# Conditioning matrix in slabs of 1024 columns, its blocks in pairs, and the head loops written out

## The reference

```python
cs = jax.nn.silu(c)
for i in range(DEPTH):
    mod = cs @ ada_w[i] + ada_b[i]                      # 9 x 12288, ada_w[i] is 2048 x 12288
    sh1, sc1, g1, sh2, sc2, g2 = jnp.split(mod, N_ADA, axis=-1)
    h = rmsnorm(x, norm_mix_g[i]) * (1.0 + sc1[:, None]) + sh1[:, None]
    out = retention(h, ...) if i == 0 else pool_mixer(h, ...)
    x = x + g1[:, None] * out
    h = rmsnorm(x, norm_ffn_g[i]) * (1.0 + sc2[:, None]) + sh2[:, None]
    x = x + g2[:, None] * swiglu(h, ffn_w_in[i], ffn_w_out[i])
return rmsnorm(x, final_norm_g), ...
```

## Time and profile before

| | us |
|---|---|
| median of 3 runs | 3572.06 (3571.36 to 3572.34) |
| the profiled execution | 3572.51 |
| its span, first to last instruction | 3570.9 |

### The profile page before, as it was taken

The page is one execution under the profiler, slowest core; times in us unless marked ns, Lnnn a source line. Parts: engine busy times, 40 slices in busy tenths (PEclk is TensorE's granted clock), DMA queues, the critical chain, the costliest instruction groups (busy, mean ns, idle before and its releaser), DMA issues.

```text
span 3570.9 us, 61767 instructions
## 1 busy us (share of the span) xinstructions
PE 3371.0 (94%) x23530; PEld 3048.3 (85%) x23530; DVE 1737.4 (49%) x2763; ACT 1068.4 (30%) x1334; POOL 105.2 (3%) x152
## 2 busy tenths in 40 slices
PE   6799999999999987999999999998499999999997
PEld 2588888888888876899999999988489999999997
DVE  0334463645537357344444444445845545455555
ACT  1233322232322223322322223323333333333332
POOL 0000000000000001000000000000100000000000
PEclk8699999999999997999999999999699999999998
DMA  9665767576675744766666666665154444454442
GB/s 330 227 222 190 252 216 251 182 252 222 212 253 195 254 173 162 243 208 211 211 211 211 212 211 212 228 219 166 59 202 152 147 148 151 147 148 152 147 149 98
DMA packets 191213, 699.63 MB, mean 196 GB/s; under 512 B 20432, under 2 KB 20688, under 8 KB 191088
## 3 DMA queue, kind: packets, MB, share of 16 engines
q1 hardware_dynamic: 170496, 619.26, 51.6%
q0 software_dynamic: 19440, 74.97, 6.2%
q10 hardware_dynamic: 1152, 3.56, 0.3%
HBM read 656.23 MB, written 41.48 MB: 195 GB/s over the span
## 4 chain that ended last, share of the span: by engine, by line
PE 88%; DVE 5%; DMA 3%; issue 2%; ACT 1%; POOL 0%; SPq 0%; DVEq 0%; POOLq 0%; ACTq 0%
PE pair L1199 27%; PE pair L1201 25%; PE pair L1200 25%; PE adab L1214 6%; DMA sb_raw<-in_ada_w 2%; DVE sb_w_lo L753 1%; PE m L1185 1%; DVE sb_big L1044 1%; PE m L1353 1%; DMA sb_raw<-in_ret_w_in 1%; PE m L1319 1%; PE m L1228 0%; PE m L1349 0%; DVE sb_X L882 0%; ACT sb_w_hi L538 0%
## 5 line engine op out<-in xcount | busy, mean ns | idle before, releaser
L753 DVE TENSOR_TENSOR sb_w_lo<-sb_raw,sb_w_hi 128x1024 fp32r<-128x1024 f32 x792 | 966.3, 1223 | 1367.9 <-ACT sb_w_hi L538 1364.8
L1199 PE MATMUL pair<-sb_h_hi,sb_w_hi 128*128 128x320 f32 x4416 | 1406.2, 318 | 50.0 <-DVE sb_h_lo L1108 32.1
L538 ACT ACTIVATE sb_w_hi<-sb_raw 128x1024 fp32r<-128x1024 f32 x792 | 837.8, 1060 | 2019.9 <-PE pair L1201 994.7
L1201 PE MATMUL pair<-sb_h_hi,sb_w_lo 128*128 128x320 f32 x4416 | 1370.8, 310 | 0.0
L1200 PE MATMUL pair<-sb_h_lo,sb_w_hi 128*128 128x320 f32 x4416 | 1370.3, 310 | 0.0
L1199 PEld LDWEIGHTS pair<-sb_h_hi,sb_w_hi 128*128 128x128 f32 x4416 | 835.8, 189 | 166.1 <-issue 119.3
L1200 PEld LDWEIGHTS pair<-sb_h_lo,sb_w_hi 128*128 128x128 f32 x4416 | 836.6, 189 | 0.0
L1201 PEld LDWEIGHTS pair<-sb_h_hi,sb_w_lo 128*128 128x128 f32 x4416 | 835.4, 189 | 0.0
L1199 PE MATMUL pair<-sb_y_hi,sb_w_hi 128*128 128x320 f32 x1920 | 602.6, 314 | 13.5 <-DVE sb_y_lo L1032 10.4
L1200 PE MATMUL pair<-sb_y_lo,sb_w_hi 128*128 128x320 f32 x1920 | 596.6, 311 | 0.0
L1201 PE MATMUL pair<-sb_y_hi,sb_w_lo 128*128 128x320 f32 x1920 | 596.3, 311 | 0.0
(11 more groups left out here) (158 smaller groups left out, 1325.5 us busy)
## 6 DMA issues: line engine op xcount, KB each, us to landing
sb_raw<-in_ada_w SPq DMA_DIRECT2D x384, 512.0 KB, 3.6
sb_raw<-in_ffn_w_in SPq DMA_DIRECT2D x352, 512.0 KB, 3.6
sb_raw<-in_ret_w_in SPq DMA_DIRECT2D x192, 512.0 KB, 4.9
sb_raw<-in_ffn_w_out SPq DMA_DIRECT2D x176, 512.0 KB, 3.6
sb_big<-in_state_ret POOLq DMA_DIRECT2D x32, 1024.0 KB, 8.7
sb_raw<-in_ret_w_out SPq DMA_DIRECT2D x64, 512.0 KB, 4.3
out_state_ret_sample<-sb_big POOLq DMA_DIRECT2D x32, 1024.0 KB, 6.4
out_state_ret_prompt<-sb_o_s POOLq DMA_DIRECT2D x8, 512.0 KB, 4.1
```

What stands on the lines that cost most here:

```text
L538: A(w_hi[s][:, :, :], raw[C.n["unit"] % RAW_SLOTS][:, :, :], ACT.Copy).then_inc(hi_done, 1)
L753: V.tensor_tensor(w_lo[s][:, :, :], raw[slot][:, :, :], w_hi[s][:, :, :].bitcast(F32), ALU.subtract)\
L1199: MM(out, wh, hi[:, c, :], start=first and k == 0, stop=False)
L1201: ins = MM(out, wl, hi[:, c, :], start=False, stop=last and k == BK - 1)
```

## The change

The conditioning matrix is laid out anew on the host (`in_slabs`): a conditioning block is now one chunk of 128 rows by 1024 columns. The four column groups take 256 columns each of the same chunk, and 16 blocks in a row complete a *slab* of 1024 columns, with no partial sums. ACT copies the bank once a slab; TensorE transposes the two halves (`turn_ada`) into the other half of the same bank; DVE adds the bias of eight chunks at once. For layer 0 shift and scale are interleaved in the first four slabs.

Conditioning blocks come in pairs behind weight blocks: behind every second one in the heads' first two laps and in the first feed-forward step of each layer (`EACH_SECOND`), behind every third one over all three laps in layer 0's steps 1 to 10 (`EACH_THIRD`). SP loads them in the order in which they are used. With `pend`, ACT copies behind its fourth split of a lap, TensorE turns behind the lap's first weight block, and DVE adds the bias behind its fifth split. In the heads this is the gate lap, in the feed-forward steps the first lap. TensorE's step F now waits for the bias addition, not the copy. The loops over heads 2 to 7 (1 to 6 on POOL) are written out on every engine. The diff, cut:

```diff
-ADA0 = 16
+SLAB = 8
+SLABS = 6 * DC // SLAB
+SLABS0 = 2 * DC // SLAB
...
+NONE = ()
+EACH_SECOND = (1, 3, 5, 7)
+EACH_THIRD = ((2, 5), (0, 3, 6), (1, 4, 7))
+
+
+def first_layer_order():
+
+    return [4 * q + (SH1, SC1)[part] + c for q in range(4) for part in range(2) for c in range(4)]
+
+
+def at_shift(c):
...
+            def load_ada(layer):
+
+                load("ada", block_of(a["ada_w"][layer], C("adas", -layer * SLABS), C.n["ada"] % DC))
+                if C.n["ada"] % DC == 0:
+                    C.n["adas"] += 1
+
+            def load_block(src, k=0, layer=0, pairs=NONE):
 
                 load("gemm", src)
-                if owed:
-                    load_ada(owed.pop())
-                if now:
-                    load_ada(ada)
-                elif ada is not None:
...
+                if k in pairs:
+                    load_ada(layer)
+                    load_ada(layer)
+
+            def load_k16(w, cols, layer=0, pairs=NONE):
                 for n in range(8):
-                    load_block(block_of(w, n % 4, cols[n // 4]), ada, now=end and n == 7)
-
-            def load_k4(w, row):
...
+            for _ in range(DC):
+                load_ada(0)
+            with C.loop(sp, 1, SLABS0, unit=DC, ada=DC, adas=1):
+                for _ in range(DC):
                     load_ada(0)
-            with C.loop(sp, 1, ADA0 // 2, unit=8, ada=8, adas=2):
-                for _ in range(8):
...
             def head(h, out):
-                load_k16(w_in, [h * 2 + VCOL // BN, h * 2 + (VCOL // BN + 1)], ada=0)
-                load_k16(w_in, [h + KCOL // BN, h + QCOL // BN], ada=0)
+                load_k16(w_in, [h * 2 + VCOL // BN, h * 2 + (VCOL // BN + 1)], 0, EACH_SECOND)
+                load_k16(w_in, [h + KCOL // BN, h + QCOL // BN], 0, EACH_SECOND)
                 load_k16(w_in, [h * 2 + GCOL // BN, h * 2 + (GCOL // BN + 1)])
                 if out:
                     load_k4(w_out, h - 1)
 
             head(0, False)
             head(1, True)
-            with C.loop(sp, 2, H, unit=48, gemm=32, ada=16, adas=4) as h:
+            for h in range(2, H):
                 head(h, True)
             load_k4(w_out, H - 1)
...
+            def feed_forward(layer, i, pairs):
                 w1, w2 = a["ffn_w_in"][layer], a["ffn_w_out"][layer]
-                load_k16(w1, [i * 2, i * 2 + 1], ada=ada)
-                if out:
-                    load_k4(w2, i - 1)
-                load_k16(w1, [i * 2 + DFF // BN, i * 2 + (DFF // BN + 1)], ada=ada, end=end)
-
-            feed_forward(0, 0, 1, out=False)
-            with C.loop(sp, 1, FF_STEPS, unit=40, gemm=24, ada=16, adas=4) as i:
-                feed_forward(0, i, 1)
+                load_k16(w1, [i * 2, i * 2 + 1], 1, pairs[0])
+                if len(pairs) == 3:
+                    load_k4(w2, i - 1, 1, pairs[1])
+                load_k16(w1, [i * 2 + DFF // BN, i * 2 + (DFF // BN + 1)], 1, pairs[-1])
+
+            feed_forward(0, 0, (EACH_SECOND, EACH_SECOND))
+            with C.loop(sp, 1, FF_STEPS, unit=40, gemm=24, ada=16, adas=1) as i:
+                feed_forward(0, i, EACH_THIRD)
...
             def copy_ada():
 
-                act.wait_ge(ada_done, C("adas") * 4 + 4)
+                act.wait_ge(ada_done, C("adas") * DC + DC)
                 if C.n["adas"]:
-                    act.wait_ge(ada_folded, C("adas"))
+                    act.wait_ge(ada_turned, C("adas"))
                 A(ada_sb[:, :], adab[:, 0:BN], ACT.Copy).then_inc(ada_copied, 1)
                 C.n["adas"] += 1
 
...
-            def lap(posts, ada=False, pend=False, ahead=0):
+            def lap(posts, pairs=NONE, pend=False, ahead=0):
 
                 for k in range(8):
                     if k >= ahead:
-                        split(with_ada(ada, k))
-                    if (k == 2 and pend) or (k == 6 and ada):
+                        split(k, pairs)
+                    if k == 3 and pend:
                         copy_ada()
...
+            def head(first=False, steps=True):
+                lap({3: [step_A] if steps else [],
                      7: ([step_B] if steps else []) + [lambda: finish_v(0)]},
-                    ada=True, ahead=AHEAD if first else 0)
+                    EACH_SECOND, ahead=AHEAD if first else 0)
                 lap({3: ([step_C] if steps else []) + [lambda: finish_v(1)],
-                     7: [step_D] if steps else []}, ada=True, pend=True)
-                lap({7: ([lambda: round_y(0), lambda: round_y(1)] if steps else []) + [lambda: finish_g(0)]},
+                     7: [step_D] if steps else []}, EACH_SECOND)
+                lap({7: ([lambda: round_y(0), lambda: round_y(1)] if steps else []) + [lambda: finish_gate(0)]},
                     pend=True)
                 if steps:
-                    lap({3: [lambda: finish_g(1)]})
+                    lap({3: [lambda: finish_gate(1)]})
                 C.n["head"] += 1
...
+            def feed_forward(pairs, ahead=0, pend=False):
+                first = len(pairs) == 2
                 lap({3: [] if first else [lambda: round_y(1)], 7: [lambda: finish_gate(0)]},
-                    ada=ada, pend=ada and not first, ahead=ahead)
+                    pairs[0], pend=pend, ahead=ahead)
                 if first:
-                    lap({3: [lambda: finish_gate(1)], 7: [lambda: round_y(0)]}, ada="end" if end else ada, pend=ada)
+                    lap({3: [lambda: finish_gate(1)], 7: [lambda: round_y(0)]}, pairs[1])
                 else:
-                    lap({3: [lambda: finish_gate(1)]}, pend=ada)
-                    lap({7: [lambda: round_y(0)]}, ada=ada)
-
-            squares_ahead(1, 3, True)
-            norm(1, mods[0], SH2, ada=True)
-            feed_forward(first=True, ada=True, ahead=AHEAD)
-            with C.loop(act, 1, FF_STEPS, unit=40, gemm=24, adas=4, y=2):
-                feed_forward(ada=True)
+                    lap({3: [lambda: finish_gate(1)]}, pairs[1])
+                    lap({7: [lambda: round_y(0)]}, pairs[2])
...
+            def take_mod(bank=adab):
+
+                dve.wait_ge(ada_turned, C("adas", 1))
+                layer = C.n["adas"] // SLABS
+                chunk = C("adas", -layer * SLABS) * SLAB
+                src = bank[:, BN:2 * BN].rearrange("p (h j n) -> p j h n", h=2, j=4)[:, :, :, 0:NC9]
+                to = mods[layer][:, bass.ds(chunk, SLAB), :].rearrange("p (j h) n -> p j h n", h=2)
+                bias = ada_bT[:, bass.ds(C("adas") * SLAB, SLAB)].rearrange("p (j h) -> p j h", h=2)
+                V.tensor_tensor(to, src, bias.unsqueeze(3).broadcast_to([P, 4, 2, NC9]), ALU.add).then_inc(mod_dve, 1)
+                C.n["adas"] += 1
+
+            def lap(posts, pairs=NONE, pend=False, ahead=0):
 
                 for k in range(8):
                     if k >= ahead:
-                        split(with_ada(ada, k))
+                        split(k, pairs)
                     for post in posts.get(k, ()):
                         post()
-                    if take and pend and k in (0, 4):
+                    if k == 4 and pend:
                         take_mod()
...
+                dve.wait_ge(mod_dve, C("adas"))
+                by = DC if n else 4
+                for c in range(0, DC, by):
+                    gate_of(mod, gain, scale_at, c, by)
...
+            def ada_block():
+
+                s, k = C.n["unit"] % RAW_SLOTS, C.n["ada"] % DC
+                pe_.wait_ge(raw_landed[s], C("unit", 0, RAW_SLOTS) * 16 + 16)
                 if k == 0 and C.n["adas"]:
                     pe_.wait_ge(ada_copied, C("adas"))
+                    if C.n["adas"] >= SLABS0:
+                        pe_.wait_ge(mod_dve, C("adas"))
                 for j in range(4):
-                    ins = MM(adab[KPAD * j:KPAD * j + KPAD, 0:BN], csT[:, 4 * k + j, :],
-                             raw[s][:, j, :], start=k == 0, stop=k == 3)
+                    ins = MM(adab[KPAD * j:KPAD * j + KPAD, 0:BN], csT[:, k, :], raw[s][:, j, :],
+                             start=k == 0, stop=k == DC - 1)
                 ins.then_inc(ada_done, 1)
+                C.n["unit"] += 1
                 C.n["ada"] += 1
-                C.n["adas"] += int(k == 3)
-
...
+                C.n["adas"] += int(k == DC - 1)
+
+            def ada_pair(k, pairs):
+                if k in pairs:
+                    ada_block()
+                    ada_block()
+
+            def turn_ada(bank=adab):
+
+                pe_.wait_ge(ada_copied, C("turned", 1))
+                if C.n["turned"]:
+                    pe_.wait_ge(mod_dve, C("turned"))
+                for h in range(2):
+                    ins = turn(bank[:, BN + P * h:BN + P * h + P], ada_sb[:, P * h:P * h + P])
+                ins.then_inc(ada_turned, 1)
+                C.n["turned"] += 1
+
+            def lap16(between=None, pairs=NONE, pend=False, fresh=None):
+
+
+                for n in range(8):
+                    k = n % 4
```

(58 more changed lines are left out.)

331 lines of the change are left out of this document (121 added, 210 removed).

## The result

The changed kernel is slower: 3767.6 us (median of 4 runs, 3756.7 to 3770.7) against 3572.2, a ratio of 1.0542 (95% interval 1.0520 to 1.0564). 3598 was forecast. The profiled execution took 3756.7 us, its span is 3754.9 against 3570.9: +184.0. It is the fastest of the four, so the medians lie 195 apart and the spans 184; what follows compares spans.

What follows compares the result with a forecast made beforehand. TensorE's own stream was taken to bound the kernel. Terms of -50 - 21 (folds) - 20 - 9 + 82 + 4 + 10 + 30 made +26 us on the 3570.9 span: 3598 us, range 3505 to 3630.

Steps and rivals of the forecast that it cites:

- pairs, a couple of weight blocks and a pair: Conditioning blocks behind the first stage: two weight blocks and a pair take 8.25 us against 8.56, -50 us in all.
- a step without its waits: Layer 0's looped feed-forward steps: 94.7 us each without the idle at the turn, a sign that the forecast is wrong.
- loops written out: Head loops as straight code: TensorE's waits for "issue" at five back edges and the half clock go, -20 us.
- first stage: Start of the kernel, 64 conditioning blocks: faster loading with fewer stops for ACT's copy, -9 us, bounds nothing to 19.
- the turn, ten steps: Feed-forward steps: TensorE idles 5.7 us for ACT's late copy and loses 2.5 to half clock, +82 us (51 to 97).
- last output lap's wait for y: Last output lap of layer 0: y is formed behind the split of a late block, some 4 us later, +4.
- couples without a step between: Some 20 couples in head 0 and two first feed-forward steps: splits late by 0.1 to 1.0 us, +10 (1 to 20).
- state loads in the heads: Heads 2 to 7: POOL's 1 MB state loads fall into weight-load bursts, 4.0 us a head and half clock, +30 (0 to 45).
- part 5: Slab ends in feed-forward steps: TensorE waits for ACT's copy, queued behind the late fourth weight block's split; ten steps, +82 us.
- part 6: Weight loads released three weight blocks ahead come late after pairs: +10 us in couples, +30 in heads 2 to 7.
- part 4's aside: Loads at a core's 358 GB/s memory share: a block every 1.46 us, the fourth 0.6 later, 6 us over ten steps.
- the two dearest rivals: Look-ahead missed everywhere in the heads, 3643 us, chance 0.08; a pair's second block as dear as a lone one, 3648, 0.05.

Runs made afterwards that it cites:

- all_early: Changed kernel with ACT's copy and silu and DVE's strip and bias additions behind earlier splits in the ten feed-forward steps; 3513.0 us, ratio 0.9830.
- small_states: Changed kernel with the four state loads of heads 1 to 7 moving 256 KB instead of 1 MB each; 3741.0 us, ratio 1.0482.

## Why the prediction was wrong

| term of the sum | forecast | measured |
|---|---|---|
| pairs, a couple of weight blocks and a pair | 8.25 us | 8.24 |
| a step without its waits | 94.7 | 95.0 (all_early) |
| loops written out | -20 | -21.8 |
| first stage | -9 | -4.6 (-2.3 to -5.2 in the other traces) |
| the turn, ten steps | +82 | +79.9 |
| last output lap's wait for y | 5.5 + 4 | 9.0 |
| couples without a step between | +10 | 9.9 of waits (2.2 there before) |
| state loads in the heads | +30 | +20.0 (small_states) |
| **silu and strips behind late splits, ten steps** | **none** | **+171.8** |

The prices were right, and the mechanisms that the sum names came; what failed is the last row. The start of the two weight blocks of a couple in the changed kernel, at the full clock, and those of a triple:

```profile
1395.35 0.42 PE L1183 MATMUL pair<-sb_h_hi,sb_w_hi 128*128 128x320 f32 x1
...
1403.59 0.42 PE L1183 MATMUL pair<-sb_h_hi,sb_w_hi 128*128 128x320 f32 x1
```

```profile
1651.90 0.42 PE L1183 MATMUL pair<-sb_h_hi,sb_w_hi 128*128 128x320 f32 x1
...
1663.65 0.42 PE L1183 MATMUL pair<-sb_h_hi,sb_w_hi 128*128 128x320 f32 x1
```

8.24 and 11.75 us: less the weight blocks and a lone conditioning block, a second one costs 0.42 and 0.39, where 0.43 had been had by halving a row at half clock.

The turn came out as part 5 had it, link by link. At T = 1675.41 (next step's first weight block) the timeline of SP and ACT, and the landing of the loads issued at 1675.29 and 1677.39:

```profile
1675.29 0.33 SPq L315 DMA_DIRECT2D sb_raw<-in_ffn_w_in  x1
1675.95 1.01 SPq L315 DMA_DIRECT2D sb_raw<-in_ada_w  x2
1677.39 4.51 SPq L315 DMA_DIRECT2D sb_raw<-in_ffn_w_in  x2
...
1683.58 1.06 ACT L540 ACTIVATE sb_w_hi<-sb_raw 128x1024 fp32r<-128x1024 f32 x1 [3.51 <-DMA sb_raw<-in_ffn_w_in]
1684.54 0.36 ACT L549 ACTIVATE sb_ada_sb<-adab 128x256 f32<-128x256 f32 x1
```

```profile
sb_raw<-in_ffn_w_in SPq DMA_DIRECT2D x1, 512.0 KB, 3.6
...
sb_raw<-in_ffn_w_in SPq DMA_DIRECT2D x1, 512.0 KB, 6.1
```

First load at T - 0.1 (forecast the same), fourth landed at T + 8.1 (7.7, at most 8.4), copy done at T + 9.5 (9.3). The mean wait is 6.4 us, the upper end of 5.1 to 6.4. The clock over the 5 us behind a turn and behind the silu:

```profile
1565.70:1570.70 5.00, 5.00 (x21) 5.00 (x22) 3.87 (x5) 1.68 (x2) 0.00 (x0) 0.55 0.00 0
1604.60:1609.60 5.00, 5.00 (x25) 5.00 (x26) 2.35 (x6) 1.06 (x1) 0.00 (x0) 0.69 0.69 280
```

5 x (1 - 0.55) = 2.2 us lost, where I took 2.5, and 1.5 behind the shorter wait. Behind the two strips' waits the same stretch shows 0.67 and 0.71.

**The step that failed** is the scope of part 5, "The new wait at the turn". It asked of *one* step, the copy, behind which split it stands, and when that split's block is loaded. That the copy was new at this place drew the question to it. But the change moved something under all the other steps too: it put pairs into the output lap, which had had no conditioning blocks, and made each third weight load wait for TensorE, where before it waited for a split far ahead. The silu and the strips stood unchanged in the diff, and the same question asked of them gives the waits at once: O3's load leaves with the pair, lands after 3.4 us, ACT's 1.06 and the silu follow, and TensorE wants the bank with no weight block between: some 5 us; the strips one block less and DVE's work more: some 4. Measured, the three waits were 12.0 us a step (4.9 and twice 3.6), and the stretches behind them in one step, at 0.69, 0.67 and 0.71, lost 4.7: 16.7 of the missing 17.2 us (120.2 - 103.0). "Less look-ahead", part 6, did treat the loads after a pair, but asked only when TensorE wants the *block*, which is late by nothing in triples, and not what stands queued behind its split. For the same reason I passed over `take_mod`: "in time, since the next slab starts two weight blocks later" holds only once the turn is late itself.

The smaller misses: the first stage gained 4.6 us (DVE's first split of a weight block starts at 113.9 for 118.5), inside its bounds and half of what I took. The state loads cost 20 and not 30: the waits that went with them in small_states were 2.7 us a head where I took 4.0 (13.7 in five heads), and no half clock came with them. The clock was still 1.00 around the longest wait of head 2, 2.2 us up to 404.65:

```profile
404.00:409.00 5.00, 4.35 (x29) 4.36 (x30) 1.83 (x3) 1.64 (x2) 0.00 (x0) 1.00 0.72 230
```

Put 172 in place of nothing, 20 for 30 and -4.6 for -9, and the sum of the prediction is +192 us against +184.0 in the span. In part 4's aside, three loads at 1.46 us in place of 1.28 put the fourth 0.5 later and not 0.6, which changes nothing. The range's upper end, 3630, left out even the two dearest rivals (3643 and 3648, 0.13 together), and the measured time is 120 us above the dearer of them: no case had a mechanism that I had found once and that acts in more places. The turn and the loops came near their terms for the reasons given, as runs show; the couples' term was a rough mean of wide bounds, and so its closeness is partly luck.

## What to carry to other kernels

When loads are reordered in a ring of few buffers, list for each load which consumer releases it, and then go through *every* instruction that stands behind that load's first use on an in-order engine, edited or not: its deadline is set by who waits for it, and its earliest time by the load. A wait found once is a pattern to be searched for. And before giving a rearrangement up, move the queued steps: here moving four kinds of step took the changed kernel from 5.4% above the kernel before to 1.7% below it (and 1.0% below the kernel before with its head loops written out, 3549.6 us).

## What the runs showed of the hardware

A load of 512 KB that left with no other in flight landed after 3.2 to 3.6 us at the places shown; over the ten steps of the changed kernel such loads took 3.0 to 3.8 us. In a burst of four the last left about 2 us after the first (1.94 to 2.10), since the issuing queue put them out some 0.65 us apart. Cutting the bytes of two of the four by three quarters brought the landing of the fourth only 1.7 us forward (8.2 us after the first's issue, then 6.5). A wait of 2.2 us in the heads left the granted clock at 1.00; over the 5 us behind waits of 3.4 to 4.9 us (strips, silu) it was 0.67 to 0.71, and behind one of 6.2 us (turn) 0.55.
